# Mixture-of-experts outputs: a scatter by matmul after each expert, or rows stored in memory and fetched by indirect DMA

## The chip, the cores and the metric

The kernel runs on one core of a Trainium2 chip. The metric is device time in microseconds (us) of one execution of the whole program.

## What is computed

The reference is a decoder trunk for one sequence of 256 tokens of width 1024, in float32: four layers of a token mixer and a channel mixer, and a final RMSNorm. The mixers are stick-breaking attention (layers 0 and 3), an S5 state-space layer (1) and latent attention (2). Layers 0 and 2 have a dense SwiGLU; layers 1 and 3 have eight expert SwiGLUs, of which each token uses two:

```python
logits = (hf @ w_router) + b_router
top_v, top_i = lax.top_k(logits, 2)
top_w = jax.nn.softmax(top_v, axis=-1)
gates = jnp.sum(one_hot(top_i, 8) * top_w[..., None], axis=1)
for e in range(8):                       # D_FF_EXPERT = 1408
    g, u = jnp.split(hf @ w_gate_up[e], 2, axis=-1)
    out = out + gates[:, e:e+1] * ((jax.nn.silu(g) * u) @ w_down[e])
x = x + out
```

## The kernel before, in words

The program is written engine by engine with semaphores; no scheduler decides an order. Every float32 product is made of three fp32r matmuls on high and low halves (`split3`, lines 284 to 286: low weights by high activations, high by low, high by high).

**Weights.** All weights of the trunk pass through one stream of pieces of up to 128x3072 elements. SyncE (SP) issues the load of a piece into one of four `raw` buffers (`load_piece`, L318) when the piece four before it has been split. ScalarE (ACT) writes the high half `whi` (`split_hi`, L329) when the load has landed and TensorE (PE) has used the piece three before it, since there are three `whi` and `wlo` buffers. VectorE (DVE) then writes the low half `wlo` (`split_lo`, L336), and PE waits for that. ACT and DVE have their splits at fixed places in their own programs.

**An expert.** An expert has twelve pieces: four column blocks j = 0 to 3 (384, 384, 384 and 256 wide) of the gate g, the up projection u and the down projection d. The order of the pieces is g0 u0 g1 u1 g2 d0 u2 g3 d1 u3 d2 d3. Each expert takes up to 128 tokens (`CAP`). `pick` is a 0/1 matrix that DVE makes from the routing; `gather` (PE, L1407, 8 matmuls) multiplies it with the tokens and `turn_tokens` (L1417) transposes the result, both for expert e+1 during expert e. `turn(j)` (L1452) transposes the block's activation, `alo` (DVE, L1672, `mlo`) makes its low half.

**The output of an expert, before.** When d3 is done the expert's 128 rows of y are in PSUM banks 4 and 5. ACT copies the high half (`yhi`, L1564), DVE makes the low half (`ylo`, L1700). After g0 and u0 of the next expert PE does `scatter(e - 1)`: 8 matmuls of `put` with `ylo` and `yhi` (L1428, L1430). It then transposes the present expert's `pick` (L1479, 2 transposes) and ACT copies it to `put` (L1548). `xadd(e - 1)` on DVE at j = 0 multiplies the scattered rows by the gates and adds them to x (L1646, and L1652 four times). Expert 0, experts 1 to 6 (a loop) and expert 7 are three copies of this code; after expert 7 come its own scatter and `xadd`. If an expert had more than 128 tokens, a branch (`rest_*`) would do the others.

GpSimd (POOL) does nothing during the experts. The MoE layers run twice, as m = 0 and m = 1; the second is the last layer, with only its final adds, the norm and the store behind it.

Of the kernel before, what the change touches and what calls it, by code (L numbers as in the profile page):

```python
# [15 lines left out]
P = 128  # L16
D = 1024
L = 256
# [85 lines left out]
def hybrid_trunk(nc, consts, x_in, norm_mix, norm_ffn, final_norm, sb_w_qkv, sb_w_o, lam_re_in, lam_im_in,  # L104
# [65 lines left out]
    with ExitStack() as ctx:  # L170
# [34 lines left out]
        def stage(*tensors):  # L205
            made = {}
            with ExitStack() as scope:
                for name, shape, dt in tensors:
# [37 lines left out]
                   ("cur", [P, 2, TT], F32), ("curg", [P, TT], F32))  # L246
        h = mo["h"]
        ov = stage(("pad_ov", [P, 8 * KB], F32), ("oT", [P, KC, P], F32), ("owg", [P, KC, P], F32),
# [12 lines left out]
        tabs = nc.dram_tensor("s5_tables", [KC, P, SLOT], F32, kind="Internal").ap()  # L261
        afd = nc.dram_tensor("s5_rows_af", [ST, 8, P], F32, kind="Internal").ap()
# [1065 lines left out]
        def s5_loads(sp):  # L1328
# [10 lines left out]
        m_wr, m_hh, m_hl, m_wh, m_wl, m_lg, m_sel, m_gd, m_ge, m_rk = (  # L1339
            sem("m_wr"), sem("m_hh"), sem("m_hl"), sem("m_wh"), sem("m_wl"), sem("m_lg"), sem("m_sel"), sem("m_gd"),  # L1340
# [3 lines left out]
        class ExpertSems:  # L1344

            def __init__(self):
# [18 lines left out]
                self.cug = sem("x_cug")  # L1365
# [4 lines left out]
        IOTA = cst[:, C_IOTA:C_IOTA + P]  # L1370

# [5 lines left out]
        def moe_pe(pe, m, n):  # L1377
            pe.wait_ge(m_wl, m + 1)
# [20 lines left out]
            def gather(e):  # L1399
                g = NE * m + e  # L1400
                pe.wait_ge(ex.pick, g + 1)
                if type(e) is int and e == 0:
                    pe.wait_ge(m_hl, TT * (m + 1))
# [18 lines left out]
            def scatter(e):  # L1422
                g = NE * m + e
                pe.wait_ge(ex.ylo, g + 1)
# [8 lines left out]
            def expert(e, first, last_e):  # L1433
# [21 lines left out]
                def down(j):  # L1455
# [46 lines left out]
            scatter(NE - 1)  # L1502
            rest_pe(pe, m)

        def moe_act(act, m, n):
            act.wait_ge(m_wr, 32 * (m + 1))
            act.activation(mo["wrh"][:], mo["wr"][:], ACT.Copy).then_inc(m_wh, 1)
            for t in range(TT):
                act.activation(mo["hh"][:, t, :], h[:, t, :], ACT.Copy).then_inc(m_hh, 1)
# [14 lines left out]
            def expert(e, last_e):  # L1524
# [10 lines left out]
                for j in range(JE + 1):  # L1535
# [9 lines left out]
                    if j == 0:  # L1545
                        sp_("u", 0)
                        act.wait_ge(ex.pt, g + 1)
                        act.activation(mo["put"][:].rearrange("p t s -> p (t s)"), PS[:, 5, 0:L], ACT.Copy)\  # L1548
                            .then_inc(ex.put, 1)
                        continue  # L1550
# [19 lines left out]
            expert(0, False)  # L1570
            with act.Fori(1, NE - 1) as e:
                expert(e, False)
            expert(NE - 1, True)
            rest_act(act, m)

        def moe_dve(dve, m, n):
            mk = [CHAIN_V[0]]

            def link(ins):
# [4 lines left out]
            dve.wait_ge(m_wh, m + 1)  # L1584
            dve.tensor_tensor(mo["wrl"][:], mo["wr"][:], mo["wrh"][:].bitcast(F32), ALU.subtract)\
                .then_inc(m_wl, 1)
            for t in range(TT):
                dve.wait_ge(m_hh, TT * m + t + 1)
                dve.tensor_tensor(mo["hl"][:, t, :], h[:, t, :], mo["hh"][:, t, :].bitcast(F32), ALU.subtract)\
                    .then_inc(m_hl, 1)  # L1590
# [51 lines left out]
            def xadd(e):  # L1642
                g = NE * m + e
                src = route[:, e, 2, :] if type(e) is int else \
                    route[:, bass.ds(e, 1), 2, :].rearrange("p a c -> p (a c)")
                dve.tensor_copy(mo["curg"][:], src).then_inc(ex.cug, 1)  # L1646
                dve.wait_ge(ex.cug, g + 1)
                for q, bank in enumerate((1, 6, 7, 4)):
                    t, half = q // 2, q % 2
                    v = x[:, t, half * 512:half * 512 + 512]  # L1650
                    dve.wait_ge(ex.sc, 4 * g + q + 1)
                    dve.scalar_tensor_tensor(out=v, in0=PS[:, bank, :], scalar=mo["curg"][:, t:t + 1], in1=v,  # L1652
                                             op0=ALU.mult, op1=ALU.add).then_inc(ex.xa, 1)

# [7 lines left out]
            def expert(e, first, last_e):  # L1662
# [12 lines left out]
                for j in range(JE):  # L1675
# [16 lines left out]
                    if j == 0 and not first:  # L1692
# [597 lines left out]
```

## Time and profile before

| | |
|---|---|
| time, median of 3 runs | 1914.23 us (1910.61, 1914.23, 1914.74) |
| the profiled execution | 1906.8 us, with a span of 1905.0 us |
| granted TensorE clock, mean of the span | 0.981 |
| PE busy / DVE / ACT / POOL | 1787.2 / 1306.0 / 998.0 / 287.0 us |
| bytes moved by DMA | 441.08 MB, mean 232 GB/s |

A busy time is the time in which an engine had an instruction in work; matmuls overlap, so the cadence (start to start) says what one costs. An idle time stands before the instruction that ended it, with what released it. The DMA share is that of 16 DMA engines; it can read a little over 1.

### The profile page before, as it was taken

What the parts mean: (1) busy time and instruction counts of PE and PEld (TensorE: products, weight loads), DVE (VectorE), ACT (ScalarE), POOL (GpSimd) and SP (SyncE); (2) the same over time, 40 slices, a digit from 0 to 9 for tenths busy, and PEclk for the clock granted to TensorE, in tenths of its full rate; (3) what the DMA queues carried; (4) which work ended last, traced back from release to release, by engine and by line L of the source; (5) the groups of instructions that cost most, each with busy time, mean ns of one, the idle gap of its engine ahead of it and who ended that gap; (6) DMA issues with size and microseconds to landing.
All of it is one profiled execution on the core that took longest, in us unless ns stands there. A gap on an engine that the chain in (4) does not pass through costs nothing.

```text
span 1905.0 us, 26914 instructions
## 1 busy us (share of the span) xinstructions
PE 1787.2 (94%) x10949; PEld 1627.4 (85%) x10949; DVE 1306.0 (69%) x1142; ACT 998.0 (52%) x874; POOL 287.0 (15%) x377
## 2 busy tenths in 40 slices
PE   6989999899899999999989999999998999999997
PEld 6978888789698888888968899998876889998886
DVE  4526788784568888888857454435425888888886
ACT  4364333333456666676635333333454766666664
POOL 4726999300000000000010000000020000000000
PEclk9999999999899999999999999999998999999999
DMA  8515797654379999899944155454603989999993
GB/s 293 191 62 173 241 304 229 245 211 156 112 256 322 331 316 339 315 315 313 329 156 133 34 183 193 155 166 159 201 19 112 319 313 331 321 314 331 322 333 115
DMA packets 242117, 441.08 MB, mean 232 GB/s; under 512 B 6080, under 2 KB 205792, under 8 KB 239984
## 3 DMA queue, kind: packets, MB, share of 16 engines
q1 hardware_dynamic: 239296, 430.37, 65.7%
q0 software_dynamic: 2736, 9.48, 1.4%
q8 instruction: 65, 1.06, 0.2%
q14 instruction: 20, 0.16, 0.0%
HBM read 426.06 MB, written 13.76 MB: 231 GB/s over the span
## 4 chain that ended last, share of the span: by engine, by line
PE 81%; DVE 11%; ACT 4%; issue 1%; DMA 1%; POOL 1%; SPq 1%; DVEq 0%; POOLq 0%; ACTq 0%
PE PS L284 22%; PE PS L286 22%; PE PS L285 22%; DVE wlo L336 4%; PE PS L1407 2%; PE PS L1452 1%; DMA t_af<-s_rows_af 1%; ACT whi L329 1%; PE PS L1417 1%; PE PS L1128 1%; PE PS L1165 1%; PE PS L1428 1%; PE PS L1430 1%; PE PS L464 1%; DVE h L438 1%
## 5 line engine op out<-in xcount | busy, mean ns | idle before, releaser
L336 DVE TENSOR_TENSOR wlo<-raw,whi 128x3072 fp32r<-128x3072 f32 (+3 forms) x279 | 857.7, 3081 | 287.1 <-ACT whi L329 286.0
L329 ACT ACTIVATE whi<-raw 128x3072 fp32r<-128x3072 f32 (+3 forms) x279 | 708.5, 2540 | 420.7 <-PE PS L286 420.0
L284 PE MATMUL PS<-wlo,hT_hi 128*128 128x384 f32 (+3 forms) x1936 | 632.9, 327 | 10.2 <-DVE alo L806 5.2
L285 PE MATMUL PS<-whi,hT_lo 128*128 128x384 f32 (+3 forms) x1936 | 625.9, 323 | 0.0
L286 PE MATMUL PS<-whi,hT_hi 128*128 128x384 f32 (+3 forms) x1936 | 625.9, 323 | 0.0
L284 PEld LDWEIGHTS PS<-wlo,hT_hi 128*128 128x128 f32 x1936 | 366.1, 189 | 22.8 <-DVE alo L806 7.0
L285 PEld LDWEIGHTS PS<-whi,hT_lo 128*128 128x128 f32 x1936 | 366.4, 189 | 3.7 <-issue 0.9
L286 PEld LDWEIGHTS PS<-whi,hT_hi 128*128 128x128 f32 x1936 | 366.3, 189 | 0.3
L284 PE MATMUL PS<-wlo,mhi 128*128 128x512 f32 x352 | 143.2, 407 | 16.4 <-DVE mlo L1672 16.4
L455 POOL TENSOR_TENSOR stat<-stat,cst 128x1 f32<-128x1 f32 x18 | 15.9, 890 | 821.0 <-DVE stat L432 815.1
L286 PE MATMUL PS<-whi,mhi 128*128 128x512 f32 x352 | 139.2, 395 | 0.0
L285 PE MATMUL PS<-whi,mlo 128*128 128x512 f32 x352 | 139.1, 395 | 0.0
L1543 ACT ACTIVATE msg<-PS 128x384 f32<-128x384 f32 x64 | 29.8, 466 | 123.5 <-PE PS L286 123.5
L284 PEld LDWEIGHTS PS<-wlo,mhi 128*128 128x128 f32 x352 | 66.2, 188 | 32.7 <-issue 19.7
L284 PE MATMUL PS<-hT_lo,whi 128*128 128x256 f32 x288 | 82.8, 287 | 7.0 <-DVE wlo L336 7.0
L285 PE MATMUL PS<-hT_hi,wlo 128*128 128x256 f32 x288 | 82.0, 285 | 0.0
L286 PE MATMUL PS<-hT_hi,whi 128*128 128x256 f32 x288 | 82.0, 285 | 0.0
L286 PEld LDWEIGHTS PS<-whi,mhi 128*128 128x128 f32 x352 | 66.1, 188 | 16.1
L285 PEld LDWEIGHTS PS<-whi,mlo 128*128 128x128 f32 x352 | 66.3, 188 | 13.0
L284 PE MATMUL PS<-wlo,ahi 128*128 128x512 f32 x176 | 72.4, 412 | 0.0
L285 PE MATMUL PS<-whi,alo 128*128 128x512 f32 x176 | 71.1, 404 | 0.0
L286 PE MATMUL PS<-whi,ahi 128*128 128x512 f32 x176 | 71.0, 404 | 0.0
(342 smaller groups left out, 2112.6 us busy)
## 6 DMA issues: line engine op xcount, KB each, us to landing
raw<-in_moe_w_gate_up SPq DMA_DIRECT2D x96, 1536.0 KB, 7.1
raw<-in_moe_w_down SPq DMA_DIRECT2D x48, 1536.0 KB, 7.0
raw<-in_ffn_w_gate_up SPq DMA_DIRECT2D x28, 1536.0 KB, 7.1
raw<-in_moe_w_gate_up SPq DMA_DIRECT2D x32, 1024.0 KB, 6.0
raw<-in_ffn_w_down SPq DMA_DIRECT2D x14, 1536.0 KB, 6.5
raw<-in_sb_w_qkv SPq DMA_DIRECT2D x12, 1536.0 KB, 7.6
raw<-in_moe_w_down SPq DMA_DIRECT2D x16, 1024.0 KB, 6.1
raw<-s_tables SPq DMA_DIRECT2D x8, 1536.0 KB, 7.3
```

What stands on the lines that cost most here:

```text
L284: pe.matmul(o, sh, mlw, start=start, stop=False, skip_group_check=True)
L285: pe.matmul(o, sl, mh, start=False, stop=False, skip_group_check=True)
L286: return pe.matmul(o, sh, mh, start=False, stop=stop, skip_group_check=True)
L329: act.activation(whi[p0 % SPL][:, 0:n], raw[p0 % RAW][:, 0:n], ACT.Copy).then_inc(hi_done, 1)
L336: dve.tensor_tensor(wlo[p0 % SPL][:, 0:n], raw[p0 % RAW][:, 0:n], whi[p0 % SPL][:, 0:n].bitcast(F32), ALU.subtract).then_inc(lo_done, 1)
L438: dve.scalar_tensor_tensor(out=h[:, t, :], in0=x[:, t, :], scalar=stat[:, 2, t:t + 1], in1=gain[:], op0=ALU.mult, op1=ALU.mult).then_inc(n ...
L464: pe.matmul(PS[:, bank, :], ident, cst[:, C_IOTA:C_IOTA + 512], start=True, stop=True, skip_group_check=True)
L1128: last = pe.matmul(PS[:, r, 64 * q:64 * q + 64], w[v, 3 - j, q, :], u[v, :, j], start=(j == 0), stop=(j == 3), skip_group_check=True)
L1165: last = pe.matmul(o[:, :, 32 * r:32 * r + 32], xx[:, c % 2, q, r, :], g[:, r, q, 1:5, :], start=(q == 0), stop=(q == 1), skip_group_check ...
L1407: last = pe.matmul(PS[:, 6 + half, :], mo["pick"][:, t, :], hx[:, t, half * 512:half * 512 + 512], start=(t == 0 and i == 0), stop=(t == T ...
L1417: last = pe.transpose(PS[:, 6 + k // 4, (k % 4) * P:(k % 4 + 1) * P], mo["gt"][:, k * P:(k + 1) * P], ident)
L1543: act.activation(mo["msg"][:, 0:w], PS[:, 0, 0:w], ACT.Silu).then_inc(ex.silu, 1)
```

## The change

The outputs of experts 0 to 6 are no longer scattered by PE. ACT copies y from PSUM to `ysb`, POOL stores `ysb` (128 rows of 4 KB) in a memory tensor `expert_rows`, and the next expert's copy waits for that store. After expert 0 DVE computes, for each token and each of its two choices, the row in `expert_rows`, and a gate that is zero where the choice is expert 7 (`where`). After the seventh store POOL issues four indirect DMAs that fetch 128 rows each into `yg`, which lies where `hh` and `hl` were. In the last expert DVE adds the fetched rows, times their gates, to x (`add_rows(0)` at j = 1, `add_rows(1)` at j = 2). Expert 7's output is still scattered and added as before, after expert 7; its `pick` is still transposed after its u0. The rest renames semaphores.

```diff
@@ moe_pe, expert
                     if j == 0:
-                        pe.wait_ge(ex.put, g + 1)
+                        if last_e:
+                            pe.wait_ge(ex.put, m + 1)
                         if not first:
-                            pe.wait_ge(ex.xa, 4 * g)
+                            pe.wait_ge(ex.yhi, g)
...
                 gate_or_up("g", 0)
                 gate_or_up("u", 0)
-                if not first:
-                    scatter(e - 1)
-                for t in range(TT):
-                    last = pe.transpose(PS[:, 5, t * P:(t + 1) * P], mo["pick"][:, t, :].bitcast(F32), ident)
-                last.then_inc(ex.pt, 1)
+                if last_e:
+                    pe.wait_ge(ex.yhi, g)
+                    for t in range(TT):
+                        last = pe.transpose(PS[:, 5, t * P:(t + 1) * P], mo["pick"][:, t, :].bitcast(F32), ident)
+                    last.then_inc(ex.pt, 1)
@@ moe_act, expert
                 used("d", JE - 1)
-                act.activation(mo["yhi"][:], psf[:, 2048:3072], ACT.Copy).then_inc(ex.yhi, 1)
-                if not last_e:
+                if last_e:
+                    act.activation(mo["yhi"][:], psf[:, 2048:3072], ACT.Copy).then_inc(ex.yhi, 1)
+                else:
+                    if not first:
+                        act.wait_ge(ex.stored, 16 * ((NE - 1) * m + e))
+                    act.activation(mo["ysb"][:], psf[:, 2048:3072], ACT.Copy).then_inc(ex.yhi, 1)
                     sp_("d", JE - 1)
@@ moe_dve
+            def where():
+                rk, off, use = mo["rk"], mo["off"], mo["use"]
+                shape = [P, TT, 2, NE]
+                for t in range(TT):
+                    for j in range(2):
+                        i = dve.tensor_scalar(oh[:, t, j, :], cst[:, C_IOTA:C_IOTA + NE], topf[:, t, j:j + 1], None,
+                                              ALU.is_equal)
+                link(i)
...
+                link(dve.tensor_tensor(off[:], off[:], use[:], ALU.mult))
+                dve.tensor_copy(mo["offi"][:], off[:]).then_inc(ex.off, 1)
+
+            def add_rows(j):
+                dve.wait_ge(ex.rows, 64 * (m + 1))
+                for t in range(TT):
+                    i = dve.scalar_tensor_tensor(out=x[:, t, :], in0=YG[:, 2 * t + j, :], scalar=mo["gy"][:, t, j:j + 1],
+                                                 in1=x[:, t, :], op0=ALU.mult, op1=ALU.add)
+                link(i)
...
                     sp_("u", j)
-                    if j == 0 and not first:
-                        xadd(e - 1)
+                    if j >= 1 and j < 3 and last_e:
+                        add_rows(j - 1)
...
-                if not last_e:
+                if last_e:
+                    dve.wait_ge(ex.yhi, g + 1)
+                    dve.tensor_tensor(mo["ylo"][:], psf[:, 2048:3072], mo["yhi"][:].bitcast(F32), ALU.subtract)\
+                        .then_inc(ex.ylo, 1)
+                else:
                     sp_("d", JE - 2)
-                dve.wait_ge(ex.yhi, g + 1)
-                dve.tensor_tensor(mo["ylo"][:], psf[:, 2048:3072], mo["yhi"][:].bitcast(F32), ALU.subtract)\
-                    .then_inc(ex.ylo, 1)
-                if not last_e:
                     sp_("d", JE - 1)
...
             expert(0, True, False)
+            where()
@@ new on POOL
+        def rows_pool(pool, m):
+            with pool.Fori(0, NE - 1) as e:
+                pool.wait_ge(ex.yhi, NE * m + e + 1)
+                pool.dma_start(y_mem.rearrange("(e p) d -> e p d", p=P)[bass.ds(e, 1)].rearrange("a p d -> (a p) d"),
+                               mo["ysb"][:]).then_inc(ex.stored, 16)
+            pool.wait_ge(ex.off, m + 1)
+            pool.wait_ge(ex.gr, NE * (m + 1))
+            pool.wait_ge(ex.stored, 16 * (NE - 1) * (m + 1))
+            for t in range(TT):
+                for j in range(2):
+                    pool.indirect_dma_start(YG[:, 2 * t + j, :], None, y_mem[:, :],
+                                            bass.IndirectOffsetOnAxis(ap=mo["offi"][:, t, j:j + 1], axis=0))\
+                        .then_inc(ex.rows, 16)
```

On PE, between the last matmuls of u0 and the first of g1 in the expert loop, the program before has:

```order
L286 MATMUL PS<-whi,hT_hi 128x384
L1428 MATMUL PS<-ylo,put 128x512
L1430 MATMUL PS<-yhi,put 128x512
L1428 MATMUL PS<-ylo,put 128x512
L1430 MATMUL PS<-yhi,put 128x512
L1428 MATMUL PS<-ylo,put 128x512
L1430 MATMUL PS<-yhi,put 128x512
L1428 MATMUL PS<-ylo,put 128x512
L1430 MATMUL PS<-yhi,put 128x512
L1479 MATMUL PS<-cst,pick 128x128 x2
L1484 ISA
L340 REGISTER_ALU
```

The same place in the program of the change (its lines 288 to 290 are 284 to 286 of before):

```order
L289 MATMUL PS<-whi,hT_lo 128x384
L290 MATMUL PS<-whi,hT_hi 128x384
L1492 ISA
L344 REGISTER_ALU
L288 MATMUL PS<-wlo,hT_hi 128x384
```

Eight matmuls and two transposes are gone there, and nothing stands in their place. On DVE, the middle of the last expert (from its second `mact` on), before:

```order
L1685 TENSOR_TENSOR mact<-PS,msg 128x384
L336 TENSOR_TENSOR wlo<-raw,whi 128x3072
L336 TENSOR_TENSOR wlo<-raw,whi 128x2048
L1672 TENSOR_TENSOR mlo<-PS,mhi 128x384
L336 TENSOR_TENSOR wlo<-raw,whi 128x3072
L1685 TENSOR_TENSOR mact<-PS,msg 128x384
L336 TENSOR_TENSOR wlo<-raw,whi 128x2048
L336 TENSOR_TENSOR wlo<-raw,whi 128x3072
L1672 TENSOR_TENSOR mlo<-PS,mhi 128x384
```

and in the change (L340, L1712, L1725 are L336, L1672, L1685 of before):

```order
L1725 TENSOR_TENSOR mact<-PS,msg 128x384
L340 TENSOR_TENSOR wlo<-raw,whi 128x3072
L1691 SCALAR_TENSOR_TENSOR x<-yg,gy,x 128x1024 x2
L340 TENSOR_TENSOR wlo<-raw,whi 128x2048
L1712 TENSOR_TENSOR mlo<-PS,mhi 128x384
L340 TENSOR_TENSOR wlo<-raw,whi 128x3072
L1725 TENSOR_TENSOR mact<-PS,msg 128x384
L340 TENSOR_TENSOR wlo<-raw,whi 128x2048
L1691 SCALAR_TENSOR_TENSOR x<-yg,gy,x 128x1024 x2
L340 TENSOR_TENSOR wlo<-raw,whi 128x3072
L1712 TENSOR_TENSOR mlo<-PS,mhi 128x384
```

The two pairs of adds of fetched rows stand ahead of the splits of g3 and of d2.

## Rows read from the trace of the kernel before

**Rows 1.** The page: busy time by engine, and DMA in 40 slices.
```profile
PE 1787.2 (94%) x10949; PEld 1627.4 (85%) x10949; DVE 1306.0 (69%) x1142; ACT 998.0 (52%) x874; POOL 287.0 (15%) x377
...
DMA  8515797654379999899944155454603989999993
```

**Rows 2.** Waits between 560 and 940 us, experts 1 to 7 of the first MoE layer.
```profile
ACT whi L329 <- PE PS L286: 50.8, 36, 2.1
...
PE PS L284 <- DVE mlo L1672: 7.2, 7, 1.0
...
PE PS L284 <- DVE wlo L336: 0.2, 1, 0.2
```

**Rows 3.** Busy time in one expert (PE, PEld, DVE, ACT, POOL, clock, DMA share, GB/s).
```profile
617.00:671.00 54.00, 52.84 (x300) 48.49 (x298) 45.88 (x31) 36.85 (x27) 0.00 (x0) 1.00 0.92 323
```

**Rows 4.** The chain of waits at the scatter of two experts: start, us, what.
```profile
642.09 0.23 PE PS L1428
...
643.91 0.22 PE PS L1479 x2
644.13 0.18 PE PS L284
...
695.88 0.23 PE PS L1428
```

**Rows 5.** Timeline in expert 1, first MoE layer: ACT, DVE, DVE, PE; and routing operations earlier.
```profile
580.51 2.77 ACT L329 ACTIVATE whi<-raw 128x3072 fp32r<-128x3072 f32 x1
...
583.95 6.77 DVE L336 TENSOR_TENSOR wlo<-raw,whi 128x3072 fp32r<-128x3072 f32 x2
590.64 0.55 DVE L1685 TENSOR_TENSOR mact<-PS,msg 128x384 f32<-128x384 f32 x1
...
594.34 0.49 PE L1452 MATMUL PS<-cst,mact 128*128 128x128 f32 x3
...
512.27 0.63 DVE L1607 TENSOR_SCALAR oh<-cst,topf 128x8 f32<-128x8 f32 x4
...
513.22 0.17 DVE L1614 RECIPROCAL gw<-gw 128x2 f32<-128x2 f32 x1
513.42 0.16 DVE L1615 TENSOR_TENSOR gw<-gw 128x2 f32<-128x2 f32 x1
```

**Rows 6.** Timeline in the last expert of the second MoE layer: DVE, then PE.
```profile
1860.46 3.35 DVE L336 TENSOR_TENSOR wlo<-raw,whi 128x3072 fp32r<-128x3072 f32 x1
...
1869.12 3.36 DVE L336 TENSOR_TENSOR wlo<-raw,whi 128x3072 fp32r<-128x3072 f32 x1 [2.30 <-ACT whi L329]
...
1872.86 2.28 DVE L336 TENSOR_TENSOR wlo<-raw,whi 128x2048 fp32r<-128x2048 f32 x1
1876.39 3.36 DVE L336 TENSOR_TENSOR wlo<-raw,whi 128x3072 fp32r<-128x3072 f32 x1 [1.25 <-ACT whi L329]
1879.67 0.55 DVE L1672 TENSOR_TENSOR mlo<-PS,mhi 128x384 fp32r<-128x384 f32 x1
...
1880.52 0.40 PE L284 MATMUL PS<-wlo,mhi 128*128 128x512 f32 x1
```

**Rows 7.** A VectorE operation with two SBUF inputs of 128x1024, and ns min/median/max.
```profile
L438 DVE SCALAR_TENSOR_TENSOR h<-x,stat,gain x18: 1277/1284/1287, 10.0 to 1900.6; 128x1024 f32<-128x1024 f32 x18
```

**Rows 8.** The copy of y in expert 6, and a POOL DMA: issue, and its kind with us to landing.
```profile
1838.07 1.03 ACT L1564 ACTIVATE yhi<-PS 128x1024 fp32r<-128x1024 f32 x1 [1.01 <-PE PS L286]
...
966.21 0.58 POOL L459 DMA_DIRECT2D gain<-in_norm_ffn  x1 [1.62 <-DVE h L438]
...
gain<-in_norm_mix POOLq DMA_DIRECT2D x4, 512.0 KB, 4.1
```

**Rows 9.** Who waited for weight loads (us, times); and two stretches of 2 us in full flow.
```profile
  ACT whi L329: 0.7, 1
...
652.00:654.00 2.00, 2.00 (x13) 2.00 (x12) 2.00 (x1) 1.17 (x1) 0.00 (x0) 1.00 1.02 412
...
728.00:730.00 2.00, 2.00 (x12) 1.71 (x11) 2.00 (x1) 0.39 (x1) 0.00 (x0) 1.00 1.06 375
```

More of the change, by code:

```diff
@@ L245, in hybrid_trunk @@
                    ("gw", [P, TT, 4], F32), ("route", [P, NE, 3, TT], F32), ("rb", [P, NE], F32), ("cmx", [P, 1], F32), ("lgt", [NE, L], F32),
-                   ("cur", [P, 2, TT], F32), ("curg", [P, TT], F32))
+                   ("cur", [P, 2, TT], F32), ("curg", [P, TT], F32), ("ysb", [P, D], F32),
+                   ("rk", [P, TT, 2], F32), ("off", [P, TT, 2], F32), ("offi", [P, TT, 2], I32),
+                   ("use", [P, TT, 2], F32), ("gy", [P, TT, 2], F32))
         h = mo["h"]
+        fetched = stage(("pad_yg", [P, TT, D], F32), ("yg", [P, 2 * TT, D], F32))
         ov = stage(("pad_ov", [P, 8 * KB], F32), ("oT", [P, KC, P], F32), ("owg", [P, KC, P], F32),
@@ L1364, in __init__ @@
                 self.cur = sem("x_cur")
-                self.cug = sem("x_cug")
+                self.stored = sem("x_st")
+                self.off = sem("x_off")
+                self.rows = sem("x_rows")
         ex = ExpertSems()
@@ L1370, in hybrid_trunk @@
         IOTA = cst[:, C_IOTA:C_IOTA + P]
+        YG = fetched["yg"]
         def moe_split(m, e, s):
@@ L1377, in moe_pe @@
         def moe_pe(pe, m, n):
-            pe.wait_ge(m_wl, m + 1)
+            pe.wait_ge(m_lo, 3 * m + 1)
             for k in range(KC):
@@ L1402, in gather @@
                 if type(e) is int and e == 0:
[L1403 removed]
+                    pe.wait_ge(m_lo, 3 * (m + 1))
                 for half in range(2):
@@ L1420, in turn_tokens, with scatter @@
                         last.then_inc(ex.g, 1)
-            def scatter(e):
-                g = NE * m + e
-                pe.wait_ge(ex.ylo, g + 1)
+            def scatter():
+                pe.wait_ge(ex.ylo, m + 1)
                 for q, bank in enumerate((1, 6, 7, 4)):
@@ L1501, in moe_pe @@
             expert(NE - 1, False, True)
-            scatter(NE - 1)
+            scatter()
             rest_pe(pe, m)
@@ L1506, in moe_act @@
             act.wait_ge(m_wr, 32 * (m + 1))
-            act.activation(mo["wrh"][:], mo["wr"][:], ACT.Copy).then_inc(m_wh, 1)
+            act.activation(mo["wrh"][:], mo["wr"][:], ACT.Copy).then_inc(m_hi, 1)
             for t in range(TT):
-                act.activation(mo["hh"][:, t, :], h[:, t, :], ACT.Copy).then_inc(m_hh, 1)
+                act.activation(mo["hh"][:, t, :], h[:, t, :], ACT.Copy).then_inc(m_hi, 1)
             act.wait_ge(m_gd, m + 1)
@@ L1522, in ghi, with expert @@
                                    ACT.Copy).then_inc(ex.ghi, 1)
-            def expert(e, last_e):
+            def expert(e, first, last_e):
                 g = NE * m + e
@@ L1546, in expert @@
                         sp_("u", 0)
-                        act.wait_ge(ex.pt, g + 1)
-                        act.activation(mo["put"][:].rearrange("p t s -> p (t s)"), PS[:, 5, 0:L], ACT.Copy)\
-                            .then_inc(ex.put, 1)
+                        if last_e:
+                            act.wait_ge(ex.pt, m + 1)
+                            act.activation(mo["put"][:].rearrange("p t s -> p (t s)"), PS[:, 5, 0:L], ACT.Copy)\
+                                .then_inc(ex.put, 1)
                         continue
@@ L1569, in moe_act @@
             ghi(0)
-            expert(0, False)
+            expert(0, True, False)
             with act.Fori(1, NE - 1) as e:
-                expert(e, False)
-            expert(NE - 1, True)
+                expert(e, False, False)
+            expert(NE - 1, False, True)
             rest_act(act, m)
@@ L1640, in pick, with xadd @@
                 i.then_inc(ex.pick, 1)
[L1642 to L1647, printed above, removed]
+            def xadd():
+                link(dve.tensor_copy(mo["curg"][:], route[:, NE - 1, 2, :]))
                 for q, bank in enumerate((1, 6, 7, 4)):
@@ L1712, in moe_dve @@
             expert(NE - 1, False, True)
-            xadd(NE - 1)
-            dve.wait_ge(ex.xa, 4 * NE * (m + 1))
+            xadd()
+            CHAIN_V[0] = mk[0]
+            dve.wait_ge(ex.xa, 4 * (m + 1))
             rest_dve(dve, m)
@@ L1831, in rest_pool @@
             with pool.If(tokens_left(pool, m)):
-                pool.wait_ge(ex.xa, 4 * NE * (m + 1))
+                pool.wait_ge(ex.xa, 4 * (m + 1))
                 with pool.Fori(0, NE) as e:
@@ L2234, in _ @@
             norm_pool(pool, 3)
+            rows_pool(pool, 0)
             rest_pool(pool, 0)
@@ L2243, in _ @@
             norm_pool(pool, 7)
+            rows_pool(pool, 1)
             rest_pool(pool, 1)
```

30 lines of the change are left out of this document (21 added, 9 removed).

## The prediction, made before the change was run

> **What bounds the kernel now.** I read the page first, then the waits of the MoE stage, then the chain, then the timeline at the two places where the change puts work, and the DMA view last, because it is the one that could speak against the change.
>
> The page shows PE busy for 94% of the span, and DMA at 90% or more in most slices of the dense and MoE stages [rows 1]. Both could be the bound. The waits decide. In experts 1 to 7 of the first MoE layer ACT waits 50.8 us for PE before its `whi` splits, that is, for PE to free a buffer; no wait of ACT for a load is listed there, and in the whole program loads made ACT wait once, for 0.7 us [rows 2, 9]. PE itself waits for `mlo` once an expert, 1.0 us each, and for `wlo` almost not at all [rows 2]. So the weight stream follows PE, and PE is the bound. In 54 us of an expert PE is busy for 52.84 us, DVE for 45.88 us, ACT for 36.85 us, and the clock is granted in full [rows 3].
>
> **What PE loses.** In the chain of waits the scatter is on the path: its first matmul begins at 642.09, the two `pick` transposes at 643.91, the next gate matmul at 644.13 [rows 4]. The 8 scatter matmuls cost 1.82 us and the transposes 0.22 us. Seven scatters per layer go (experts 0 to 6; that of expert 7 stays) and seven pairs of transposes (experts 0 to 6), in two layers: 14 x 1.82 = 25.5 us and 14 x 0.22 = 3.1 us, together 28.6 us of PE time. From scatter to scatter an expert takes 695.88 - 642.09 = 53.79 us [rows 4], so a middle expert should take 51.75 us.
>
> Is the next piece ready when PE comes 2.04 us earlier? DVE loses `ylo`, the small copy and four adds per expert, so it is not later than before. The 1.0 us wait for `mlo` at the end of an expert is a chain turn, ACT, DVE that starts on PE and moves with it: it stays. ACT has the same 1.03 us copy (to `ysb` in place of `yhi`) and loses a copy to `put`. Its new wait for the previous store costs nothing: the store has a whole expert, some 50 us, and the nearest row for 512 KB issued by POOL is 0.58 us of issue and 4.1 us to landing [rows 8].
>
> **What DVE gains, first place: `where()`, before expert 1.** Four comparisons take 0.63 us as the same ones in the routing do, then seven linked small operations at 0.20 us each (513.22 to 513.42 is one) and an unlinked one: about 2.2 us [rows 5]. `whi` of g1 ends at 580.51 + 2.77 = 583.28 [rows 5], so the `wlo` of g1 ends near 586.6, `where` near 588.8, the `wlo` of u1 near 592.2 and `mact` near 592.7. `turn(0)`, which needs that `mact`, was at 594.34 and would be at 592.30. PE loses about 0.4 us, twice: 0.8 us. Bounds: 0, if the small operations overlap more, and 2.2 us a layer if none of it is covered.
>
> **Second place: `add_rows`, in expert 7.** Two SBUF-input operations of 128x1024 take 1.284 us each [rows 7], 2.57 us a pair. In expert 7 PE keeps its transposes, so everything behind u0 comes 1.82 us earlier. I write new times on the clock of before, less 1.82. The `wlo` of u2 ends at 1860.46 + 3.35 - 1.82 = 1861.99, so the first pair ends at 1864.56. Then come the `wlo` of g3 and `mlo`, until about 1867.35. The `wlo` of d1 waited for ACT until 1869.12, now 1867.30: caught up. The `wlo` of u3 ends at 1872.86 + 2.28 - 1.82 = 1873.32, the second pair at 1875.89. The `wlo` of d2 could have begun at 1876.39 - 1.82 = 1874.57, so it is 1.32 us late, and with it the `mlo` behind it, which ended at 1879.67 + 0.55 = 1880.22, only 0.30 us ahead of PE's `down(2)` at 1880.52 [rows 6]. So PE waits about 1.0 us there, in each layer: 2.0 us. Bounds: 0 to 5.1 us a layer (both pairs uncovered).
>
> **POOL and the fetch.** Nothing is queued behind POOL's waits in the MoE stage but the branch test and the next norm's power, which come after the stage. The last store is issued after the copy at 1838.07, which ends at 1839.10; with 0.6 + 4.1 us it has landed at 1843.8 [rows 8]. The rows are needed when DVE reaches `add_rows(0)`, 1861.99. So the four fetches have 18.2 us, 4.5 us each if they went strictly one after another. No row shows an indirect DMA. The bounds are 0.6 us each plus one landing (6.5 us in all) and some twice the 4.7 us of a whole 512 KB POOL DMA, one after another (38 us). I take the near end, since the plain POOL DMA of the same 512 KB is the nearest row. Cost: nothing; the cover is the 18.2 us.
>
> **Bytes.** An expert's weights are 3 x 1024 x 1408 x 4 B = 17.30 MB, its store 0.52 MB: 17.8 MB in 51.75 us is 344 GB/s, against 323 before [rows 3]. Stretches in full flow moved 375 to 412 GB/s [rows 9], and at 375 an expert needs 47.5 us. Expert 7 has 2.1 MB of fetches in place of its store: 19.4 MB, 51.7 us at 375, just what PE takes. The four buffers carry that. Cost taken: nothing.
>
> The Trainium skill speaks against this: SBUF — State Buffer, in "A bandwidth-pool intuition that's wrong (but worth ruling out)", gives about 358 GB/s between HBM and a core. The trace disagrees, with 375 to 412 GB/s in full flow [rows 9]. By the page's figure expert 7 would need 54.2 us, some 2.2 us over PE's, and the sum would lose 4.4 us more (an estimate from that page): about 1893.
>
> **The sum.** 28.6 - 0.8 - 2.0 = 25.8 us. The profiled execution would go from 1906.8 to 1881.0 us. It is 7.4 us below the median of the runs, which I take to be the same offset after: 1914.2 - 25.8 = **1888.4 us**, 1.3% faster. About 0.2% (4 us) is what a measurement of this kernel can tell from no change.
>
> **The rivals.**
> - *Expert 7 bound by loads.* The fetches take 2.1 MB / 0.375 to 0.412 = 5.1 to 5.6 us of the DMA engines. If nothing absorbs this, each layer loses 5.4 us: gain 15.0, 1899. For it: that stretch has no room at 375 GB/s. Against: four buffers, and ACT waits 50.8 us for PE, over 1 us a split [rows 2]. The skill's figure above makes it likelier, but the rows stand against that figure. Chance 0.13.
> - *Fetched rows late.* If a fetch takes 8 us and they go one after another, they land at 1843.8 + 32 = 1875.8, 13.8 us late. DVE stands in `add_rows(0)` with the splits of g3, d1, u3 and d2 behind it, so PE stops for nearly as long: 2 x 13.3 = 26.6, no gain, 1915. The point from which it costs is 4.5 us each. Against: the near rows. Chance 0.08.
> - *The DMA engines are the real bound, slower than before.* If the 323 GB/s of now were the ceiling, 17.8 MB would take 55.2 us, 1.4 us more than now: 14 x 1.4 = 20, and two fetches of 2.1 MB 13 us: 1947. It decides from the point at which 344 GB/s can't be had. For it: the slices at 9 [rows 1]. Against: 412 GB/s in a stretch, and no ACT wait for a load [rows 9]. Chance 0.04.
> - *The change does not do what it says*: PE's time goes but returns as a wait at the same place, since something I take to move with PE does not. Then 1914. Against: `whi` and `wlo` of g1 are ready over 1 us ahead. Chance 0.03.
>
> **How the numbers follow.** The forecast has 0.72, from 1882 (no stall, and 2 to 3 us of spread between runs) to 1893. With the first rival it makes 0.85. The range of 1882 to 1901 takes both in and leaves out about 0.15 to 0.2. Faster: 0.72 + 0.13 and a part of the second rival, 0.88. Same: 0.05. Slower: the third rival and a fetch beyond 8 us, 0.07.
>
> **What would show it.** Right: period of a middle expert 51.7 to 51.8 us; no PE matmul between u0 and g1; DMA share near 0.97 with ACT still waiting for PE and not for `raw`; PE waits of about 0.4 us in expert 1 and 1.0 us ahead of `down(2)` in expert 7; `yg` landed before `add_rows(0)` with DVE not idle there. Wrong: ACT `whi` waiting for `raw`; DVE idle before L1691 on a DMA; an expert period above 52.5 us.

## The result, and the profile after

| | before | after |
|---|---|---|
| time, median | 1913.51 us (4 runs, 1910.61 to 1914.74) | **1898.49 us** (4 runs, 1895.88 to 1900.04) |
| ratio | | 0.9925, 95% interval 0.9912 to 0.9938 |
| profiled execution, span | 1906.8 us, 1905.0 us | 1895.88 us, 1894.4 us |
| granted TensorE clock, mean | 0.981 | 0.976 |

The change gains 15.0 us (0.8%; by the interval 11.9 to 16.8). A second timing beside other runs of the kernel before gave a ratio of 0.9943 (0.9929 to 0.9956). The forecast was 25.8 us. The time lies in the range, but at the figure of the first rival.

The page after; its first line answers to [rows 1]:

```profile
PE 1767.2 (93%) x10809; PEld 1611.2 (85%) x10809; DVE 1260.7 (67%) x1090; ACT 994.6 (53%) x860; POOL 313.9 (17%) x399
...
DMA  8515787754369999999944155454513899999993
...
q0 software_dynamic: 5904, 21.02, 3.0%
```

PE lost 20.0 us of busy time between these two traces. The next window is one middle expert after; it answers to the window of [rows 3]. Columns as there: PE, PEld, DVE, ACT, POOL busy, granted clock, DMA share, GB/s.

```profile
635.76:687.49 51.73, 50.58 (x285) 46.59 (x285) 42.02 (x26) 36.37 (x24) 0.54 (x1) 1.00 0.97 345
```

That is the forecast's step to the digit: 51.7 us, DMA share 0.97. The other parts of the program show where the missing gain went. The table cuts each trace at the start of the copy of y (`yhi` before, `ysb` after), the one event of an expert that both kernels have. Expert 0 starts at the first copy of gathered tokens.

| us | start to expert 0 (layer 1) | expert 0 | 1 | each of 2 to 6 | 7 | copy of 7 to expert 0 of layer 3 | expert 0 | 1 | 2 to 6 | 7 | rest |
|---|---|---|---|---|---|---|---|---|---|---|---|
| before | 521.1 | 58.47 | 53.78 | 53.8 | 51.12 | 504.0 | 57.97 | 53.80 | 53.8 | 51.12 | 15.8 |
| after | 525.1 | 58.36 | 52.27 | 51.72 | 53.71 | 506.3 | 58.12 | 52.26 | 51.72 | 55.07 | 16.0 |

Expert 1 takes 0.54 us more than a middle one. Expert 7, which should have taken 51.12 - 1.82 + 1.0 = 50.3 us, takes 53.7 and 55.1. Here are POOL, ACT, DVE and PE in expert 7 of the second MoE layer. The columns are start, duration, operation, and in brackets the idle time before it with what ended it.

```profile
1825.05 0.53 POOL L1772 DMA_DIRECT2D expert_rows<-ysb  x1 [51.18 <-ACT ysb L1578]
1833.36 2.01 POOL L1779 DMA_INDIRECT yg<-expert_rows,offi  x1 [7.78 <-DMA expert_rows<-ysb]
1835.68 3.48 POOL L1779 DMA_INDIRECT yg<-expert_rows,offi  x1 [0.30 <-issue]
1839.47 0.94 POOL L1779 DMA_INDIRECT yg<-expert_rows,offi  x1 [0.30 <-issue]
1840.71 3.12 POOL L1779 DMA_INDIRECT yg<-expert_rows,offi  x1 [0.30 <-issue]
...
1841.49 2.78 ACT L333 ACTIVATE whi<-raw 128x3072 fp32r<-128x3072 f32 x1 [1.48 <-DMA raw<-in_moe_w_gate_up]
1847.16 1.91 ACT L333 ACTIVATE whi<-raw 128x2048 fp32r<-128x2048 f32 x1 [1.51 <-DMA raw<-in_moe_w_gate_up]
1853.27 2.77 ACT L333 ACTIVATE whi<-raw 128x3072 fp32r<-128x3072 f32 x1 [3.82 <-DMA raw<-in_moe_w_down]
...
1851.91 2.48 DVE L1691 SCALAR_TENSOR_TENSOR x<-yg,gy,x 128x1024 f32<-128x1024 f32 x2 [4.25 <-DMA yg<-expert_rows,offi]
1854.43 2.29 DVE L340 TENSOR_TENSOR wlo<-raw,whi 128x2048 fp32r<-128x2048 f32 x1
...
1856.87 0.55 PE L288 MATMUL PS<-wlo,hT_hi 128*128 128x256 f32 x1 [3.02 <-DVE wlo L340]
1857.22 0.41 PE L289 MATMUL PS<-whi,hT_lo 128*128 128x256 f32 x1
1857.43 0.41 PE L290 MATMUL PS<-whi,hT_hi 128*128 128x256 f32 x1
```

Both of the first two rivals are in these rows: ACT waits for weight loads, and DVE waits for the fetched rows. Which of them costs the time, the trace alone doesn't say, since PE's 3.02 us stand behind DVE, which was late for the rows, while ACT was late too. Over the program the view of the `whi` line after lists ACT's idle time for loads, which was 0.7 us before [rows 9]:

```profile
  PE PS L290: 410.6, 127
  DMA raw<-in_moe_w_gate_up: 12.6, 10
  DMA raw<-in_moe_w_down: 6.9, 3
```

Windows of expert 7 in the second layer, first after, then before (columns as above):

```profile
1830.00:1834.00 4.00, 4.00 (x25) 3.96 (x24) 3.35 (x2) 2.94 (x2) 0.64 (x1) 1.00 1.04 424
1842.00:1846.00 4.00, 4.00 (x25) 3.83 (x25) 3.65 (x4) 2.76 (x2) 1.83 (x1) 1.00 1.05 385
1854.00:1858.00 4.00, 1.13 (x5) 1.16 (x6) 3.96 (x4) 3.78 (x2) 0.00 (x0) 0.72 1.07 395
1858.00:1862.00 4.00, 4.00 (x21) 4.00 (x20) 4.00 (x3) 0.17 (x1) 0.00 (x0) 0.50 0.79 282
```

```profile
1845.00:1849.00 4.00, 4.00 (x23) 3.64 (x22) 3.89 (x2) 2.94 (x2) 0.00 (x0) 1.00 1.01 384
...
1853.00:1857.00 4.00, 4.00 (x26) 4.00 (x25) 3.64 (x7) 3.53 (x3) 0.00 (x0) 1.00 1.08 372
1857.00:1861.00 4.00, 4.00 (x25) 4.00 (x24) 4.00 (x4) 2.78 (x1) 0.00 (x0) 1.00 0.57 221
```

Before, the DMA engines were full from 4 to 20 us behind the copy of y (share 1.01 to 1.08), had some room after that (0.57 from 1857 to 1861, then up to 0.96), and moved next to nothing from 36 us on (shares of 0.02 and less). The changed program closes that gap by its own speed, before any fetch is added. Here are three windows of the kernel without fetch (its experiment is below); they begin 24, 28 and 36 us behind its copy of y:

```profile
1847.21:1851.21 4.00, 4.00 (x21) 3.55 (x20) 2.76 (x2) 2.08 (x3) 0.00 (x0) 1.00 1.07 280
1851.21:1855.21 4.00, 4.00 (x30) 4.00 (x29) 2.79 (x1) 2.58 (x2) 0.00 (x0) 1.00 1.01 411
...
1859.21:1863.21 4.00, 4.00 (x28) 3.63 (x27) 3.52 (x2) 2.73 (x3) 0.00 (x0) 1.00 0.00 0
```

There the share is 0.99 to 1.09 in every window of 4 us from 4 to 32 us. The fetch, issued 10 us behind the copy of y, is put into the full part. In the first list, the windows of expert 7 after, the third and fourth show something more: after PE's 3.02 us stall its granted clock is 0.72 and then 0.50, that is, its lower level of 1.2 GHz, with 128x256 matmuls 0.21 us apart.

### The profile page after: what moved, and what is told of

Same layout as the page of the kernel before. It is cut to its first block, busy times and chain, and to the rows that moved or that the text cites. A ratio compares the mean times of both kernels' runs of the same rounds, so it can differ in the third digit from the quotient of the medians.

```text
span 1894.4 us, 26590 instructions
## 1 busy us (share of the span) xinstructions
PE 1767.2 (93%) x10809; PEld 1611.2 (85%) x10809; DVE 1260.7 (67%) x1090; ACT 994.6 (53%) x860; POOL 313.9 (17%) x399
## 3 DMA queue, kind: packets, MB, share of 16 engines
q8 instruction: 64, 1.05, 0.2%
## 4 chain that ended last, share of the span: by engine, by line
PE 74%; DVE 12%; ACT 4%; DMA 4%; issue 3%; POOL 1%; SPq 1%; DVEq 0%; POOLq 0%; ACTq 0%
PE PS L288 21%; PE PS L290 20%; PE PS L289 20%; DVE wlo L340 5%; DMA t_af<-s_rows_af 2%; PE PS L1415 2%; ACT whi L333 1%; PE PS L1459 1%; PE PS L1169 1%; PE PS L1132 1%; SPq L1325 1%; DVE h L442 1%; PE PS L468 1%; DMA raw<-in_moe_w_down 1%; PE PS L1425 1%
## 5 line engine op out<-in xcount | busy, mean ns | idle before, releaser
L340 DVE TENSOR_TENSOR wlo<-raw,whi 128x3072 fp32r<-128x3072 f32 (+3 forms) x279 | 857.4, 3080 | 309.8 <-ACT whi L333 309.2
L288 PE MATMUL PS<-wlo,mhi 128*128 128x512 f32 x352 | 143.3, 407 | 17.3 <-DVE mlo L1712 17.3
L1772 POOL DMA_DIRECT2D expert_rows<-ysb x14 | 7.5, 536 | 767.6 <-ACT ysb L1578 767.6
```

What stands on the lines that cost most here:

```text
L288: pe.matmul(o, sh, mlw, start=start, stop=False, skip_group_check=True)
L340: dve.tensor_tensor(wlo[p0 % SPL][:, 0:n], raw[p0 % RAW][:, 0:n], whi[p0 % SPL][:, 0:n].bitcast(F32), ALU.subtract).then_inc(lo_done, 1)
```

## The experiments

**Theory 1**: the bytes of the fetch crowd the weight loads, so the weights land late in `raw` and the chain ACT, DVE, PE is late. **Theory 2**: the fetched rows are late for `add_rows(0)` and DVE stands there with four splits behind it. A third question is whether something outside the experts was lost.

### The kernel before again, and the kernel after again

No edit; one execution each, for the spread of the stages.

> The kernel before, unchanged, for a second trace. Outside the MoE stages the first trace of the change was 6.3 us longer than the first trace of before: 2.0 us in each stick-breaking attention stage (first norm to second norm 147.7 against 149.7; 138.8 against 142.8 less what lies between), 2.0 in the stage that makes the S5 tables. Theory 1: these stages vary from one execution to the next, whatever the kernel; then this trace differs from the first one of before by 1 to 4 us there. Theory 2: the change costs this time (where its tensors and code lie); then this trace repeats the first one of before within 0.5 us in each stage. Experts 1 to 7 take 53.8, and the last 51.1 us, by both.

> The changed kernel, unchanged, for a second trace. Middle experts 51.7 us, the last one 53.7 to 55.1 us as before. Theory 1 (the stages outside vary by themselves): these differ from the first trace of the change by 1 to 4 us. Theory 2: they repeat within 0.5 us.

Measured: 1907.86 and 1900.32 us. Expert stages repeat within 0.6 us in both. Between the two MoE layers, before took 504.1 us again (504.0), and after 510.8 us (506.3 the first time). So what lies outside the experts varies by several us.

### No fetch; and neither store nor fetch

```diff
-                    if j >= 1 and j < 3 and last_e:
-                        add_rows(j - 1)
...
-            pool.wait_ge(ex.stored, 16 * (NE - 1) * (m + 1))
-            for t in range(TT):
-                for j in range(2):
-                    pool.indirect_dma_start(YG[:, 2 * t + j, :], None, y_mem[:, :],
-                                            bass.IndirectOffsetOnAxis(ap=mo["offi"][:, t, j:j + 1], axis=0))\
-                        .then_inc(ex.rows, 16)
```

The rows of experts 0 to 6 are neither fetched nor added to x (VectorE waits for the stores ahead of its last adds); the second kernel also leaves the stores out (POOL's `dma_start` of `ysb` and ACT's wait on `ex.stored`).

> Leaves out the four indirect DMAs and the adds of fetched rows, so the outputs of experts 0 to 6 are missing from x; the stores stay. Theory 1: the last expert is long (53.7 and 55.1 us from copy of y to copy of y, against 49.3 that I expected without stalls) only because of the fetch; then it takes 49.3 us here in both layers, ACT waits for no load there, and the kernel is 10 us faster than the change, about 1888 us. Theory 2: part of it comes from elsewhere (the store of expert 6, the missing scatter): then the last expert stays above 50 us.

> As no_fetch, and the seven stores of a layer are left out too; ACT still copies y out of PSUM. Theory 1: the stores are hidden: middle experts stay at 51.72 us, the last at 49.3 us, total as no_fetch within 2 us; ACT's few waits for loads in middle experts (2.4 us in all) go. Theory 2: the stores crowd the weight loads; then the middle experts get shorter than 51.7 us, or the total falls by over 3 us against no_fetch.

Measured: **1886.38 us**, ratio 0.9859 (0.984 to 0.9879), and 1883.81 us, ratio 0.9851 (0.9834 to 0.9867). Expert 7 takes 49.29 and 49.28 us without the fetch, just 1.83 us less than before's 51.12. So fetch and adds cost 4.4 us in the first MoE layer and 5.8 us in the second, together 10.2 us. The stores cost the middle experts nothing: 51.72 against 51.73 us. They are not without effect, though. The same `whi` view of the two kernels, without fetch and without both:

```profile
  PE PS L290: 417.2, 133
  DMA raw<-in_moe_w_gate_up: 5.3, 4
  DMA raw<-in_moe_w_down: 0.8, 1
```

```profile
  PE PS L290: 424.0, 137
  DMA raw<-in_sb_w_qkv: 0.7, 1
```

With the stores ACT waits for loads five times, without them once; neither costs the experts time. Whether the 2.6 us between the medians belong to the stores isn't settled, since the intervals overlap.

### The adds late in expert 7

`add_rows(0)` goes from j = 1 to j = 3, behind that block's `mact`, and `add_rows(1)` to the end of the expert. Both are reached later than the rows land. The fetch is issued as before.

```diff
                     if j == JE - 1:
+                        if last_e:
+                            add_rows(0)
                         alo(j)
                     sp_("u", j)
-                    if j >= 1 and j < 3 and last_e:
-                        add_rows(j - 1)
...
                 if last_e:
+                    add_rows(1)
```

> The changed kernel, unchanged, timed on the same chip as the three below: 1898 us; the last expert 53.7 to 55.1 us. Outside the MoE stages the stretch between the two (copy of y of the first layer's last expert to the first gathered tokens of the second layer) took 504.0 us in both traces of before and 506.3 to 510.8 us in the four traces of changed kernels, with a granted clock of 0.90 to 0.93 in places that had 1.00. Theory 1: which level the clock has there depends on when a stage comes, so it differs from one execution to the next between about 504 and 511 us. Theory 2: it is fixed for a kernel.

> The two pairs of adds of fetched rows are moved to the end of the last expert: one between mact(3) and mlo(3), where VectorE was idle for 2.9 us, one ahead of its wait for the copy of y. Everything is computed. The fetch is issued as before. Theory 1 (two losses: VectorE held by late rows, and weight loads crowded by the fetch): only the first goes; ACT still waits 4 to 8 us for loads in each last expert, and it takes 51 to 52.5 us, total about 1894 us. Theory 2 (only the rows' lateness matters): the last expert takes 49.3 us, total 1888 us.

Measured on the same chip: after 1898.94 us, ratio 0.9943 (0.9929 to 0.9956); adds late 1899.68 us, ratio 0.9953 (0.9939 to 0.9967). No gain. Expert 7 takes 54.29 and 55.37 us, so both figures of the expectation missed, 51 to 52.5 us and 49.3. ACT, DVE and PE there:

```profile
1855.55 4.79 ACT L333 ACTIVATE whi<-raw 128x3072 fp32r<-128x3072 f32 x2 [3.89 <-DMA raw<-in_moe_w_down]
...
1858.36 3.36 DVE L340 TENSOR_TENSOR wlo<-raw,whi 128x3072 fp32r<-128x3072 f32 x1 [4.29 <-ACT whi L333]
1861.63 0.55 DVE L1725 TENSOR_TENSOR mact<-PS,msg 128x384 f32<-128x384 f32 x1
...
1862.24 0.90 PE L1459 MATMUL PS<-cst,mact 128*128 128x128 f32 x3 [3.31 <-DVE mact L1725]
```

DVE no longer waits for rows, but for ACT, and ACT for the load of d1; PE stalls for 3.31 us, where it was 3.02 in the changed kernel. The lateness of the rows is no cause of its own: its wait was real, and ran beside the wait for the load. With it gone, the late loads cost as much.

### The fetch late as well; and `where` late too

POOL waits for DVE's `wlo` of u2 ahead of its four fetches, so they begin with the last two weight loads of expert 7, 24 us behind the copy of y and not 10. In the second kernel `where` also moves, to j = 0 of expert 7.

```diff
+            pool.wait_ge(lo_done, base[f"moe{m}"] + MOE_PIECES * (NE - 1) + NX["u", 2] + 1)
             for t in range(TT):
```

```diff
+                    if j == 0 and last_e:
+                        where()
...
-            where()
```

> As adds_late, and POOL waits for the low half of u2 of the last expert before it issues the fetch, so that the fetch runs beside two weight loads that have time, and not beside five. Theory 1: ACT's waits for loads in the last expert go, it takes 49.3 us in the last layer and up to 2 us more in the first MoE layer (where VectorE still splits a piece of the next stage there), total about 1889 us. Theory 2 (the lost time has another source): no better than adds_late.

> As fetch_and_adds_late, and the row numbers are computed by VectorE in the last expert, after the split of g2, and not before expert 1. Theory 1: expert 1 takes 51.72 us instead of 52.26, the last expert stays, since VectorE waited 1.4 us there for ACT; 1 us less in all, which a timing can hardly show and the traces can. Theory 2: the 0.55 us of expert 1 has another source and stays.

Measured: **1890.6 us**, ratio 0.989 (0.9875 to 0.9905), and **1888.29 us**, ratio 0.9889 (0.9874 to 0.9904). In the second MoE layer expert 7 is back at 49.33 and 49.30 us: the whole loss of 5.8 us is gone with the same bytes, moved by some 14 us. In the first MoE layer expert 7 takes 50.79 and 53.53 us. There the next layer's weights follow in the stream: in the first kernel the DMA share is 1.02 to 1.07 from 20 to 48 us behind the copy of y. ACT in that place of the first kernel:

```profile
936.93 2.77 ACT L333 ACTIVATE whi<-raw 128x3072 fp32r<-128x3072 f32 x1 [3.77 <-DMA raw<-in_mla_w_in]
```

`where` itself took 2.1 us (906.75 to 908.84). With it gone, expert 1 took 51.82 us in one layer but 52.21 in the other, so `where` explains only a part of the 0.54 us; the rest is open. The expectation that the last expert stays failed in the first layer, by 2.7 us. PE stalled there for 2.86 us with a granted clock of 0.50 in the 4 us behind it, in the first kernel for 2.54 us with 1.00. Whether moving `where` did that is not shown.

### Plain DMAs; and half the bytes

Both have the adds late. The first fetches fixed rows 0 to 511 with four plain DMAs in place of the routed rows. The second fetches and adds only the rows of the first 128 tokens.

```diff
-                    pool.indirect_dma_start(YG[:, 2 * t + j, :], None, y_mem[:, :],
-                                            bass.IndirectOffsetOnAxis(ap=mo["offi"][:, t, j:j + 1], axis=0))\
-                        .then_inc(ex.rows, 16)
+                    k = 2 * t + j
+                    pool.dma_start(YG[:, k, :], y_mem[k * P:(k + 1) * P, :]).then_inc(ex.rows, 16)
```

```diff
-            for t in range(TT):
+            for t in range(1):
```

> As adds_late, but the four indirect DMAs are four plain DMAs of the same 512 KB each, of the rows 0 to 511 of the stored outputs, so the added rows are not those of the tokens. Theory 1 (bytes: 2.1 MB in a stretch in which the DMA engines are already in full flow): the last expert takes 54.3 and 55.4 us as in adds_late, within 1 us. Theory 2 (the indirect form is what costs): it takes under 52 us.

> As adds_late, with only the two indirect DMAs and the adds of the first 128 tokens; the second 128 tokens lack the outputs of experts 0 to 6. Theory 1 (bytes): half of the 1.05 MB goes into the small room that the loads leave, the last expert takes 50.5 to 52.5 us. Theory 2 (a fixed price of having a fetch there, through the queue or the first DMA's wait): over 53.5 us.

Measured: 1890.65 us and 1892.84 us, one execution each. Expert 7 takes 53.94 and 53.23 us with plain DMAs (54.29 and 55.37 with indirect ones), and 50.36 and 50.26 us with half the bytes, just under the 50.5 to 52.5 of its Theory 1. Plain DMAs take POOL 2.10 us for all four:

```profile
1828.85 2.10 POOL L1781 DMA_DIRECT2D yg<-expert_rows  x4 [7.63 <-DMA expert_rows<-ysb]
```

So it is mostly the bytes: of 5.0 and 6.1 us over 49.28, plain DMAs of the same size keep 4.7 and 3.9. The rest, 0.4 and 2.1 us, would be the indirect form, from one execution each; the 0.4 is no more than expert 7 of the changed kernel varies by (53.71, 54.05 and 53.74 us in three traces), and the 2.1 is outside the 1 us that Theory 1 allowed. The total of the plain fetch is lower by more than that, since this execution was also 5.2 us shorter outside the experts than the one with adds late. The cost is not proportional: 1.05 MB costs 1.0 us, 2.1 MB four to six.

### The fetch placed by layer

As with fetch and adds late, but in the first MoE layer the fetch waits only for the low half of d0, in the hope of room ahead of the next layer's weights.

```diff
-            pool.wait_ge(lo_done, base[f"moe{m}"] + MOE_PIECES * (NE - 1) + NX["u", 2] + 1)
+            pool.wait_ge(lo_done, base[f"moe{m}"] + MOE_PIECES * (NE - 1) + NX[("d", 0) if m == 0 else ("u", 2)] + 1)
```

> The kernel before for a third trace. The stretch between the MoE stages was 504.0 and 504.1 us in the first two, and 506.3, 510.8, 509.9, 506.5, 506.3, 510.0, 511.9 and 507.8 us in eight traces of changed kernels. Theory 1 (it varies with the clock's level whatever the kernel): this trace can be anywhere from 504 to 511 us. Theory 2 (the changed kernels are slower there): 504 us again. A third 504 speaks for theory 2 without proving it.

> As fetch_and_adds_late, but in the first MoE layer POOL issues the fetch after the low half of d0 (some 5 us earlier), ahead of the loads of the next stage, for one of which ACT waited 3.8 us there. Theory 1: that wait goes and the first MoE layer's last expert takes 49.3 to 50 us instead of 50.8, the second layer's stays at 49.3; total 1 us below fetch_and_adds_late, 1889 us. Theory 2: the earlier fetch crowds the loads of u3 and d2 and gives it back: 51 us or more.

Measured: before 1909.78 us, and 1889.03 us for the fetch placed, ratio 0.988 (0.986 to 0.9899). The second layer is at 49.33 us again; the first is worse than with either place, 55.02 us, as its Theory 2 had it:

```profile
928.82 2.77 ACT L333 ACTIVATE whi<-raw 128x3072 fp32r<-128x3072 f32 x1 [2.89 <-DMA raw<-in_moe_w_down]
...
935.60 0.77 PE L288 MATMUL PS<-wlo,mhi 128*128 128x512 f32 x1 [2.68 <-DVE mlo L1712]
```

The third trace of before took 507.0 us between the MoE layers, where two had shown 504.0 and 504.1. The changed kernels have 506.3 to 512.0 there. So before is not fixed at 504, but lies at the low end.

The three kernels with the late fetch (1888.3 to 1890.6 us) compute everything and are faster than before by ratios of 0.988 to 0.989, which is 1.1 to 1.2%. The two that were timed beside the changed kernel are faster than it too (0.989 and 0.9889 against 0.9943, with intervals that don't meet). The three can't be told from one another.

## Why the prediction was right and wrong, step by step

**What bounds the kernel, and what PE loses: right.** The middle experts went from 53.8 to 51.72 us (51.75 forecast), with ACT's copy waiting for PE alone. PE's 28.6 us are there: without fetch and stores the ratio of 0.9851 is 28.5 us (by the interval 25.4 to 31.7). In the middle experts no other engine took anything back.

**`where` before expert 1: right in size.** 0.54 us a layer for 0.4, 1.1 us in all for 0.8. Moving `where` away gave back 0.45 us in one layer and 0.05 in the other.

**"POOL and the fetch": the sizes were wrong, and the cost was masked.** The forecast priced a store at 4.1 us to landing and an indirect DMA at 0.6 us of issue by the nearest rows [rows 8]. The view of the store's line after, and then that of the instructions on `yg`:

```profile
DMA to landing us min/median/max: 7.2/7.4/7.5
```

```profile
L1779 POOL DMA_INDIRECT yg<-expert_rows,offi x8: 941/2656/3484, 904.2 to 1840.7; - x8
```

The store took 7.2 to 7.5 us among the weight loads; the row of 4.1 us is the median of four loads at other places of the program, of 3.6 to 7.5 us. From the first indirect DMA to the end of the fourth POOL took 10.5 us (1833.36 to 1843.83), not 2.4. The rows were there at 1851.9, after a DVE wait of 4.25 us. The time of POOL goes with VectorE's splits. These are DVE's rows beside the four indirect DMAs above:

```profile
1834.95 3.36 DVE L340 TENSOR_TENSOR wlo<-raw,whi 128x3072 fp32r<-128x3072 f32 x1
1839.66 3.36 DVE L340 TENSOR_TENSOR wlo<-raw,whi 128x3072 fp32r<-128x3072 f32 x1 [1.36 <-ACT whi L333]
```

The indirect DMA from 1835.68 begins inside the first of these splits and ends at 1839.16, 0.85 us behind it; that from 1840.71 ends 0.81 us behind the second; that from 1839.47 begins ahead of the second and takes 0.94 us. The forecast had no such wait in it. The second rival therefore happened in kind (rows late, DVE idle before L1691), but with adds late it was gone and nothing was gained.

**"Bytes": the step that failed.** It averaged over the expert: 19.4 MB in 51.7 us at 375 GB/s, "The four buffers carry that", cost nothing. Two things were wrong with it. By the forecast's own other steps PE needed 50.3 us for expert 7, not 51.7, so at 375 GB/s the room was already 1.4 us short. And the average hides the place. Loads run four buffers ahead of their use, so part of expert 7's weights moves in expert 6: its own 51.12 us moved 216 GB/s before, 11.0 MB of the 17.3, nearly all in the first 36 us. With PE at its new speed the DMA engines are full from 4 to 32 us (0.99 to 1.09 without the fetch). The fetch came at 1833 to 1852, 10 to 28.5 us behind the copy of y. In the 30 us from 1828 to 1858 the DMA engines moved 385 GB/s; in the same place of expert 7 without the fetch they moved 352 (1827.85 to 1857.85), and before 333 (1842.7 to 1872.7). That is an estimate of 1.0 MB more for 2.1 MB of fetched rows, so the loads fell behind by the rest; ACT waited 1.48, 1.51 and 3.82 us. In the kernel with fetch and adds late the same bytes began 14 us later, behind all but the last two weight loads, and the loss in the second layer was gone. That shows that the place of the bytes is what cost the time there.

The Trainium skill, SBUF — State Buffer, in "A bandwidth-pool intuition that's wrong (but worth ruling out)", gives about 358 GB/s between HBM and a core. No run here bears it out: after moved 424, 385 and 395 GB/s in windows of 4 us, and 385 over 30 us. The forecast worked out from it that expert 7 would lose 2.2 us a layer; its own figures give 54.2 - 51.7 = 2.5. It lost 4.4 and 5.8 us at a higher rate, so a low ceiling is not what happened. The Trainium skill, HBM Reference, in "Specifications (TRN2)", gives about 425 GB/s for a core that streams alone. The 424 GB/s of one window agrees with that.

**"Second place: `add_rows`": the stall is there as forecast, where PE has its full clock.** These are DVE and PE ahead of `down(2)` in expert 7 of the first MoE layer:

```profile
932.84 2.47 DVE L1691 SCALAR_TENSOR_TENSOR x<-yg,gy,x 128x1024 f32<-128x1024 f32 x2
935.35 3.36 DVE L340 TENSOR_TENSOR wlo<-raw,whi 128x3072 fp32r<-128x3072 f32 x1
938.62 0.55 DVE L1712 TENSOR_TENSOR mlo<-PS,mhi 128x384 fp32r<-128x384 f32 x1
...
939.32 0.47 PE L288 MATMUL PS<-wlo,mhi 128*128 128x512 f32 x1 [0.94 <-DVE mlo L1712]
```

PE waited 0.94 us where 1.0 was forecast. In the second layer of this trace, where PE was slowed behind its 3.02 us stall, no such wait shows; `after_timed` has 0.93 us in both layers. It is a part of the 10.2 us.

**A term that no step had: the clock.** In the second layer PE stalled for 3.02 us and then had a granted clock of 0.72 and 0.50 in the two windows that follow. It is tempting to put the second layer's larger loss (5.8 against 4.4 us) down to that, but another trace of the same kernel, `after_timed`, speaks against it. There the same stall kept the full clock:

```profile
1855.14 0.35 PE L288 MATMUL PS<-wlo,hT_hi 128*128 128x256 f32 x1 [2.92 <-DVE wlo L340]
...
1855.14:1859.14 4.00, 3.11 (x24) 2.90 (x24) 4.00 (x4) 1.29 (x1) 0.00 (x0) 1.00 0.97 353
```

Expert 7 took 54.80 us in that trace, where it took 55.07 with the drop. So the drop cost at most 0.3 us here: at full clock PE stalls 1.00 and 0.93 us more further on. What differs between the layers in both traces is when the rows land, 27.2 us behind the copy of y in the first layer and 28.5 in the second, and PE's first stall is longer by the same 1.4 us. With adds late a difference of 1.1 us between the layers stays, so the rows are not all of it. Why the second layer loses more is open.

**The sum.** 28.6 - 1.1 - 10.2 = 17.3 us; measured were 15.0 (11.9 to 16.8), and 10.8 in the second timing (1909.78 - 1898.94; by the interval 8.4 to 13.6). What is left lies in the stretches outside the experts, which were some 6 us longer in the first trace after (525.1 and 506.3 against 521.1 and 504.0). Whether the change makes them longer stays open. For it: all eleven traces of changed kernels have 506.3 to 512.0 us between the layers, two of three traces of before 504. From the start to expert 0 of the first MoE layer the three traces of before have 521.1 to 522.2 us, the eleven of changed kernels 520.8 to 526.0. Against: the third trace of before, 507.0 between the layers, and the timing without store and fetch, whose whole gain is PE's sum. The traces do show a place where such a difference arises, the attention of layer 3. The same stretch before and without fetch (clock and DMA share at the end):

```profile
1373.00:1393.00 20.00, 15.38 (x107) 12.07 (x108) 7.07 (x8) 17.22 (x22) 5.28 (x14) 1.00 0.47 159
```

```profile
1366.00:1386.00 20.00, 14.62 (x91) 11.16 (x89) 7.58 (x8) 15.65 (x19) 3.78 (x10) 0.91 0.46 159
```

These instructions are the same in both kernels, though the second window begins 1.1 us earlier in them. From the first matmul behind the 2.56 us wait for `vv` to the one behind the 0.88 us wait for `sp`, PE took 12.89 us before (1374.79 to 1387.68) and 14.55 without the fetch (1368.86 to 1383.41). So the lower clock costs 1.7 us there, of 5.9 us between these two traces.

**The chances.** The first rival, expert 7 bound by loads, was given 0.13 and came true, at 1899 almost to the digit. That is partly luck: it took 5.4 us a layer as bytes over rate, and the loss was 4.4 and 5.8 by way of loads that came late one after another. "Against: four buffers" was the weak argument: half the bytes cost 1.0 us, the whole four to six. Two signs that the forecast had named as showing it wrong came: ACT waited for `raw` (19.5 us against 0.7), and DVE stood idle before L1691 on a DMA. The time lies in the range only because the range took in that rival; the main figure was 10 us off.

## What to carry to other kernels

Judge added DMA bytes by the rate of the few microseconds in which they will move, in a table of short windows, not by the mean of a stage; and price a transfer by a row from a stretch as crowded as the one it will run in. If the bytes have no deadline, hold their issue back until the stream thins out: here that was worth some 8 us without removing a byte. When two waits end at nearly the same place, take one away before you blame it.

## What the runs showed of the hardware that was not expected

- An indirect DMA of 128 rows of 4 KB kept POOL for 0.94 to 3.58 us, a plain one of the same bytes for 0.53 us. In eight traces with 60 of them, all 37 that took over 1.1 us had begun while a `wlo` split of VectorE had been in work for at least 0.36 us, and ended 0.80 to 0.93 us behind its end. The 23 that took 0.94 to 1.05 us began with no split in work, or within 0.04 us of its start. The place did not tell them apart: with `where` late the four took 2.84, 0.97, 0.94 and 2.96 us, with fetch and adds late 1.05, 1.81, 0.94 and 0.94, both some 24 us behind the copy of y. The four plain DMAs were issued across a split and took 2.10 us together.
- A store of 512 KB took 7.2 to 7.5 us to landing among full weight loads; the POOL load of 512 KB in [rows 8] took 4.1. A load and a store may differ as well; no run separates that.
- The length of a single stall did not tell whether PE's granted clock fell. In expert 7 the 4 us behind a stall showed 0.50 after 3.02, 3.31, 2.86 and 2.68 us, 0.57 after 2.09, 0.59 after 2.88 and 2.87, and 0.63 after 3.12, but 1.00 after 2.92, 2.54 and 2.17 us, and after all of up to 1.66 us.
- One core moved up to 424 GB/s in a window of 4 us, and 385 GB/s over 30 us, with all the stalls described above.
